# Two heads' value products on the column halves of TensorE in the forgetting attention of a two-block transformer kernel

## What is computed

```
logits[t,s] = q[t].k[s]/8 + F[t] - F[s]   for s <= t,  F = cumsum(log sigmoid(forget logit))
p = softmax(logits);  o_fox = p @ v       (8 heads of 64)
o = concat(rmsnorm(merge_heads(o_fox)) * fox_out_g, rmsnorm(merge_heads(o_sb)) * sb_out_g)
x = x + o @ w_out
```

## Time and profile before

| | |
|---|---|
| median of 3 runs | 1642.62 us (1642.62 to 1642.76) |
| profiled execution | 1642.03 us, span 1640.2 us |
| TensorE busy | 1612.2 us (98%), 7584 matmul and 7584 load instructions |
| VectorE busy | 884.7 us (54%) |
| ScalarE busy | 637.8 us (39%) |
| GpSimd busy | 239.3 us (15%) |
| mean granted TensorE clock | 0.999 |

### The profile page before, as it was taken

The page is one execution under the profiler, slowest core; times in us unless marked ns, Lnnn a source line. Parts: engine busy times, 40 slices in busy tenths (PEclk is TensorE's granted clock), DMA queues, the critical chain, the costliest instruction groups (busy, mean ns, idle before and its releaser), DMA issues.

```text
span 1640.2 us, 19220 instructions
## 1 busy us (share of the span) xinstructions
PE 1612.2 (98%) x7584; PEld 1275.2 (78%) x7584; DVE 884.7 (54%) x1447; ACT 637.8 (39%) x1089; POOL 239.3 (15%) x216
## 2 busy tenths in 40 slices
PE   7999999999999999999999999999999999999998
PEld 5567788876767888888888888786788888888887
DVE  6556455756477455334343325578555677777322
ACT  4332124446455333223322222457563344444222
POOL 1323302400031234110110203000013200000000
PEclk9999999999999999999999999999999999999999
DMA  7121113221211332332333322421103232332322
GB/s 272 44 77 39 52 50 110 90 65 54 77 49 42 129 103 79 101 103 91 102 94 99 97 97 73 167 65 39 53 1 103 91 96 86 96 97 90 128 91 77
DMA packets 39733, 142.12 MB, mean 87 GB/s; under 512 B 4531, under 2 KB 5299, under 8 KB 39260
## 3 DMA queue, kind: packets, MB, share of 16 engines
q1 hardware_dynamic: 39644, 140.89, 26.6%
HBM read 138.76 MB, written 2.11 MB: 86 GB/s over the span
## 4 chain that ended last, share of the span: by engine, by line
PE 88%; DVE 4%; POOL 3%; ACT 2%; issue 2%; DMA 1%; SPq 0%; POOLq 0%; ACTq 0%; DVEq 0%
PE ps L406 85%; PE ps L409 3%; POOL sqs L2147 2%; POOL sqt L2145 1%; DMA wraw<-in_ws 1%; ACT whi L1558 1%; DVE wlo L916 1%; DVE uT L1080 0%; DVE uT L1078 0%; DMA x<-in_x 0%; PE ps L902 0%; ACT PT L1883 0%; ACT zb L1868 0%; DVE raw L1129 0%; POOL small L2039 0%
## 5 line engine op out<-in xcount | busy, mean ns | idle before, releaser
L916 DVE TENSOR_TENSOR wlo<-wraw,whi 128x1024 fp32r<-128x1024 f32 (+2 forms) x244 | 303.7, 1248 | 452.4 <-ACT whi L1558 451.8
L406 PE MATMUL ps<-hThi,whi 128*128 128x512 f32 x1128 | 455.9, 404 | 0.0
L406 PE MATMUL ps<-hThi,wlo 128*128 128x512 f32 x1128 | 440.7, 391 | 0.0
L406 PE MATMUL ps<-hTlo,whi 128*128 128x512 f32 x1128 | 440.1, 390 | 0.0
L1558 ACT ACTIVATE whi<-wraw 128x1024 fp32r<-128x1024 f32 (+2 forms) x244 | 252.4, 1039 | 482.4 <-PE ps L406 453.9
L406 PEld LDWEIGHTS ps<-hThi,whi 128*128 128x128 f32 x1128 | 212.4, 188 | 59.8 <-issue 19.1
L406 PEld LDWEIGHTS ps<-hThi,wlo 128*128 128x128 f32 x1128 | 212.1, 188 | 45.6
L406 PEld LDWEIGHTS ps<-hTlo,whi 128*128 128x128 f32 x1128 | 212.5, 188 | 44.6 <-issue 3.6
L406 PE MATMUL ps<-whi,hThi 128*128 128x512 f32 (+1 forms) x224 | 86.7, 387 | 0.0
L406 PE MATMUL ps<-whi,hTlo 128*128 128x512 f32 (+1 forms) x224 | 84.1, 376 | 0.0
L406 PE MATMUL ps<-wlo,hThi 128*128 128x512 f32 (+1 forms) x224 | 83.9, 375 | 0.0
(11 more groups left out here) (310 smaller groups left out, 2431.4 us busy)
## 6 DMA issues: line engine op xcount, KB each, us to landing
wraw<-in_ws SPq DMA_DIRECT2D x236, 512.0 KB, 3.5
x<-in_x SPq DMA_DIRECT2D x4, 512.0 KB, 4.9
x<-in_x SPq DMA_DIRECT2D x1, 2048.0 KB, 10.0
Fb<-forget_rows SPq DMA_DIRECT2D x1, 2048.0 KB, 8.3
out<-ys SPq DMA_DIRECT2D x8, 256.0 KB, 2.4
w<-in_w SPq DMA_DIRECT2D x2, 512.0 KB, 11.5
dec<-in_dec SPq DMA_DIRECT2D x1, 1024.0 KB, 14.1
wraw<-in_ws SPq DMA_DIRECT2D x4, 256.0 KB, 2.6
```

The lines of the kernel that those rows point to most:

```text
L406: return t.matmul(o, l, r, start=first, stop=last)
L916: v.tensor_tensor(wlo[h][:, 0:width(i)], wraw[h][:, 0:width(i)], whi[h][:, 0:width(i)].bitcast(F32), ALU.subtract).then_inc(lo_done[h], 1)
```

## The change

Value products of two heads (units u and u+1) are made together: `fv` of a head (64 columns) is the stationary operand, the 128 columns of its `PTf` block move, and the heads write partitions 0 to 63 and 64 to 127 of the bank. Features now stand on the partitions. When the eight heads of a row block are through, ScalarE copies the bank (`heads_out`, into `W5[q % 3]`), and TensorE turns its four blocks of 128x128 back (`back`, into bank 6, 7, 6 and 1), before the row sums are applied as before. The last `back`, of row block 1, stands beside the output matrix. In TensorE's step, `turn` and `values` go ahead of `scores`. In ScalarE's, `evac` goes ahead of `shares`. `values` waits for the copies of both units. The norm's steps move by one step or so.

```diff
             def values(u):
+
                 n, h = pairs[u]
                 b = 6 if n > 1 else 7
-                w.wait_ge(x_ea if u % 2 else x_ev, u // 2 + 1)
+                w.wait_ge(x_ev, u // 2 + 1)
+                w.wait_ge(x_ea, u // 2 + 1)
                 w.wait_ge(fv_c, 4)
                 if h == 0:
                     take(b)
                 for k in range(n + 1):
-                    op = mm(ps[b][:, h * 64:(h + 1) * 64], PTf[u % 4][:, k * 128:(k + 1) * 128], fv[:, k, h * 64:(h + 1) * 64],
-                            k == 0, k == n)
-                op.then_inc(x_pv, 1)
-                if h == 7:
-                    free[b] = [(x_nv, 2 * (13, 15, 29, 31).index(u) + 2)]
+                    for i in range(2):
+                        op = mm(ps[b][64 * i:64 * i + 64, h * 64:h * 64 + 128], fv[:, k, (h + i) * 64:(h + i + 1) * 64],
+                                PTf[(u + i) % 4][:, k * 128:(k + 1) * 128], k == 0, k == n)
+                        if k == n:
+                            op.then_inc(x_pv, 1)
+                if u == 30:
+                    free[b] = [(o_c, 8)]
+
+            def back(q, b):
+
+                w.wait_ge(o_c, 5 + q)
+                if b == 1:
+                    take(b)
+                for k in range(4):
+                    op = across(b, k, W5[q % 3][:, k * 128:(k + 1) * 128])
+                op.then_inc(x_bk, 1)
+                free[b] = [(x_nv, 2 * q + 2)]
 
             for u in range(38):
                 while u == 3 and not fox_go:
                     yield
+                if 3 <= u < 35:
+                    turn(u - 3)
+                if u in (7, 23, 27):
+                    out_norm_turn({7: 3, 23: 4, 27: 5}[u], 3)
+                if u in (19, 21, 35):
+                    back((19, 21, 35).index(u), 7 if u == 21 else 6)
+                if u >= 6 and u % 2 == 0:
+                    values(u - 6)
                 if u < 32 and u % 2 == 0:
                     scores(u)
-                if 3 <= u < 35:
-                    turn(u - 3)
-                if u in (7, 22, 26):
-                    out_norm_turn({7: 3, 22: 4, 26: 5}[u], 3)
-                if 5 <= u < 37:
-                    values(u - 5)
-                yield
+                yield
+            flow.later(1, lambda: back(3, 1))
             flow.later(1, lambda: out_norm_turn(6, 3))
             flow.later(2, lambda: out_norm_turn(7, 3))
...
-                w.wait_ge(x_pv, u + 1)
+                w.wait_ge(x_bk, q + 1)
                 w.wait_ge(o_sc, 3 * (4 + q))
                 w.wait_ge(o_sq, 4 + q)
...
-                if u in (23, 27):
-                    out_norm_low(4 + u // 27, 4, "gfox", 3)
-                if u - 5 in (13, 15, 29, 31):
-                    q = (13, 15, 29, 31).index(u - 5)
-                    shares(q, (3, 0, 2, 1)[q])
-                yield
+                if u in (24, 28):
+                    out_norm_low(4 + u // 28, 4, "gfox", 3)
+                if u in (19, 21, 35):
+                    q = (19, 21, 35).index(u)
+                    shares(q, (3, 0, 2)[q])
+                yield
+            flow.later(1, lambda: shares(3, 1))
...
+            def heads_out(q, u):
+
+                w.wait_ge(x_pv, u + 1)
+                if q == 3:
+                    w.wait_ge(x_bk, 1)
+                a.activation(W5[q % 3][:], ps[7 if q % 2 else 6][:], ACT.Copy).then_inc(o_c, 1)
+
+            def finished(q):
+                w.wait_ge(x_nv, 2 * q + 2)
+                out_norm_square(4 + q)
+
             for u in range(38):
                 while u == 3 and not fox_go:
                     yield
+                if 3 <= u < 35 and (u - 3) % 2:
+                    evac(u - 3)
                 if u < 32:
                     shares(u)
-                if 3 <= u < 35 and (u - 3) % 2:
-                    evac(u - 3)
...
-                if u in (22, 26):
-                    out_norm_high(4 + u // 26, 4, "gfox", 3)
-                if u - 5 in (13, 15, 29, 31):
-                    q = (13, 15, 29, 31).index(u - 5)
-                    w.wait_ge(x_nv, 2 * q + 2)
-                    out_norm_square(4 + q)
+                if u in (23, 27):
+                    out_norm_high(4 + u // 27, 4, "gfox", 3)
+                if u in (18, 20, 34, 36):
+                    heads_out((18, 20, 34, 36).index(u), u - 5)
+                if u in (19, 21, 35):
+                    finished((19, 21, 35).index(u))
                 yield
             flow.later(1, lambda: out_norm_high(6, 4, "gfox", 3))
+            flow.later(1, lambda: finished(3))
...
-                if u in (5, 20, 24, 36):
-                    out_norm_scale({5: 3, 20: 4, 24: 5, 36: 6}[u])
+                if u in (5, 21, 25, 37):
+                    out_norm_scale({5: 3, 21: 4, 25: 5, 37: 6}[u])
```

More of the change, by code:

```diff
@@ L343, in build @@
         sem(n) for n in ("s_qk", "s_z", "s_ab", "s_ln", "s_sc", "s_sum", "s_tr", "s_ev", "s_pv"))
-    x_qk, x_mx, x_ex, x_tr, x_ea, x_ev, x_pv, x_nv = (
-        sem(n) for n in ("x_qk", "x_mx", "x_ex", "x_tr", "x_ea", "x_ev", "x_pv", "x_nv"))
+    x_qk, x_mx, x_ex, x_tr, x_ea, x_ev, x_pv, x_bk, x_nv = (
+        sem(n) for n in ("x_qk", "x_mx", "x_ex", "x_tr", "x_ea", "x_ev", "x_pv", "x_bk", "x_nv"))
     o_c, o_sq, o_sc, o_tr, o_hi, o_lo = (sem(n) for n in ("o_c", "o_sq", "o_sc", "o_tr", "o_hi", "o_lo"))
@@ L1411, in shares @@
                 u = (13, 15, 29, 31)[q]
-                c, b = 48 + 8 * n, 6 if n > 1 else 7
+                c, b = 48 + 8 * n, (6, 7, 6, 1)[q]
                 w.wait_ge(x_ex, u + 1)
```

## The result

Over 22 runs each, the changed kernel takes a median of 1646.86 us (1645.28 to 1649.89) and the kernel before 1642.72 us (1642.04 to 1649.03). The ratio is 1.0022, 95% interval 1.0016 to 1.0028: the change costs 3.6 us (2.6 to 4.6), at the edge of what a measurement here can tell. The two medians lie 4.1 us apart. The forecast was 1645.2, at +2.6. The profiled execution took 1646.58 us, 0.3 under the median.

A forecast was written before the change was run, and what follows sets the result against it. TensorE was taken to bound the kernel; only the 42.76 us forgetting-attention stretch could change much. Work -3.7, turning-back waits +4.1, lead +1.3 and +1.3, old waits gone -0.4: +2.6 on 1642.62, so 1645.2 us, range 1640.5 to 1649.5.

The forecast's parts named there:

- Work on TensorE: Forgetting attention: cheaper value instructions, less group steps and 16 added transposes, net -3.7 us.
- The waits at the turning back: Steps 19, 21 and 35: TensorE waits for ScalarE's row block copy 1.46, 1.80 and 0.84 us, together 4.1.
- The fourth turning back: Last row block's transposes, between output weight products: the copy is done by then, so no wait; 0.44 us of work.
- The shorter lead: TensorE asks for turns sooner after scores: waits of 1.3 us in the first half and 1.3 in the second.
- Covered turnings back: Rival: copies reach TensorE in time, so only work counts; 1638.9 us, or some 1640 with part of the lead; chance 0.10.
- Only the waits at the turning back: Rival: the shorter lead costs nothing and only the turning-back waits count; 1642.6 us; chance 0.12.
- ScalarE and VectorE set the pace: Rival: at every odd turn, half a microsecond more in each of seven cycles; about 1648.7 us; chance 0.20.
- Halves that do not overlap: Rival: in value groups, column halves hide nothing, 160 instructions cost 17.6 us in place of 8.8; 1654.0 us; chance 0.03.

The follow-up runs named there:

- scores first: Changed kernel with TensorE issuing scores ahead of turn, back and values, and ScalarE's odd copy behind the exponential again: stretch 45.01 us, ratio 1.0038 to the kernel before.
- one head after the other: Changed kernel with the loops of values swapped, all key blocks of the first head, then the second: stretch 46.99 us, ratio 1.0044 to the kernel before.
- the 67 us run: Changed kernel with ScalarE's odd-unit copy again behind the exponential, TensorE in its new order: stretch 66.95 us, 1668.22 us in one run.

## Why the prediction was right

- **Work on TensorE, -3.7 us.** Held in kind, 0.6 too large in size. 0.055 per instruction held for groups of 16, 12, 8 and 4, and the reason that the forecast gave for it, the overlap of the two halves, is what the single starts show. The steps were under-counted. From start to start, those ahead of the sixteen groups come to 1.8 us, thirteen of 0.147 before scores to 1.9, three behind the others to 0.45: 4.1 us, where the old order paid 1.0 at the same seams. That is 3.1 us more, not 2.5. I had taken 0.10 for the old step before scores from one row; that was a group of eight, and behind the small groups of the old order it was 0.05. All told the change's work is 3.1 us less, with the 0.44 beside the output matrix counted in.
- **The waits at the turning back, 4.1 us.** 1.36, 1.72 and 0.80 us against 1.46, 1.80 and 0.84, together 3.9. The chain of the first: from the copy's start to TensorE's was 1204.75 - 1204.12 = 0.63 us, where I had 0.59 + 0.15; the other links fit within 0.05. Moving the copy alone took 2.18 us out, so the cause of the first two is shown. That of the third, where the copy follows the last value product directly, rests on the rows; with the transposes behind the last value group instead, 0.29 us of idle time was left of 0.72.
- **The fourth turning back, covered.** Right: no idle time before it, and 0.4 us of work.
- **The shorter lead, 1.3 + 1.3 us.** First half 0.73 + 0.36 and 0.15 in the next wide cycle: 1.24. That the low part of the norm makes the first 1.1 is shown by its move. The place was partly wrong: I had put the wait on turn(9) alone, but turn(8) took two thirds of it. Its bank is emptied by VectorE's copy of unit 6 (L1425), which stands behind the same low part. In the second half the sum held, 1.2 us, but not the places: 0.32 at turn(24) (1216.58 to 1217.17), 0.38 at turn(28), 0.34 at turn(29), 0.12 at turn(31) and 0.05 at turn(23), where I had named 23, 25, 27, 29 and 31.
- **The sum.** For the stretch the terms give 42.76 - 4.2 + 4.1 + 2.6 - 0.4 = 44.9 us, measured 45.13: 0.6 too little in steps, 0.4 too much in waits. That these two nearly cancel is luck. The time was 1.7 us over the forecast, 1646.86 against 1645.2, of which the profiles from the stretch on explain 0.2; the ratio's interval is 1 us to either side. Most of the rest goes with the lower mean clock of ten runs: the 12 others have a median of 1645.77, 3.1 us above the kernel before.
- **The rivals.** Covered turnings back: excluded by the rows. Only the waits at the turning back, the lead for nothing: excluded as well, the lead cost 2.4 us, and moving the low part alone took 1.43 out. ScalarE and VectorE set the pace: waits of that kind came in some cycles, not in all seven, so it did not decide; the median between that case and mine is no evidence for it. Halves that do not overlap: they do, at 0.055 us for an instruction where both halves are at work against 0.109 where one is.

What stays open: how the 0.10 to 0.15 us at a change of tile shape divides between the two instructions that meet there, why the early part of this program differs from run to run, and whether the change has a part in it: ten of its 22 runs had the lower mean clock, where it was five of 25 and six of 21 in two sets of runs of the kernel before. The times of scores first and of one head after the other lie about 3 us further above the kernel before than their stretches do (ratios of 1.0038 and 1.0044, stretches 2.25 and 4.23 longer), with three of seven and three of four runs at the lower clock; their readings rest on the stretches.

## What to carry to other kernels

A cheaper instruction form is worth its price only if nothing new waits: here 3.1 us of saved work was outweighed by 6.3 us of waits, and the stretch lost 4.6 us again by reordering the queues alone. When TensorE asks for something that another engine must still copy, look at what stands ahead of that copy in the engine's queue, and put the copy of data that is ready ahead of the operation that still has to wait for its input. When groups of instructions are reordered, count the changes of tile shape between neighbours as well: with scores first they cost nearly 2 us, most of what that order saved in waits.

## What the runs showed of the hardware

- Two heads on the two halves of the columns, in fp32 with 64 stationary and 128 moving columns: each half takes an instruction every 0.109 us, and with both at work it is 0.055 us per instruction, the two starts 0.007 us apart. A head's instructions may stand up to four in a row without loss (groups of eight with the loops swapped); with six or eight in a row the second head started four before the first one's last, and the others ran alone. The old form of 128 stationary and 64 moving columns took 0.105.
- Between items of different tile shape TensorE loses 0.10 to 0.15 us more than the instructions themselves, and it does so on each side of a value group (0.11 ahead on average, 0.147 behind, before scores).
- Waits of up to 2 us before odd transposes, with 17 of 67 us idle, came with a granted TensorE clock of 0.50 in one 8 us piece and a mean of 0.85 over the 67; waits of 1.4 and 1.7 us within 6 us of each other, in the change, left it at 1.00, and so did one of the 1.97 us waits of the 67 us run. It was 1.00 again from 1240 to 1249.41, with waits of 1.51 and 1.05 us in it, and in the dense output products behind them. The lost clock cost 9.4 us, nearly as much as the waits that brought it.
